# A state space scan regrouped by four tokens, inside a two-mixer transformer kernel on Trainium2

## What is computed

```python
mag, ang = exp(a_re * dt), a_im * dt            # 32 groups of 64 complex states
lb_re, lb_im = mag * cos(ang), mag * sin(ang)
bu = einsum('bsgh,gph->bsgp', u, bb)            # bb complex, made of lb, a and b
state[t] = lb * state[t - 1] + bu[t]            # complex, for 256 tokens t
y = einsum('bsgp,ghp->bsgh', re(state), c_re) - einsum(..., im(state), c_im) + d_skip * u
y = gelu(y); y = y * sigmoid(y @ w_glu + b_glu)
mix = concat([rmsnorm(y), rmsnorm(attention)]); x = x + rmsnorm(mix @ w_out)
```

## Time and profile before

| | |
|---|---|
| Median of 3 runs | 1364.04 us (1362.24 to 1364.82) |
| The profiled execution, its own time | 1365.96 us |
| Its span, first to last instruction | 1364.0 us |
| Mean granted TensorE clock | 0.977 |
| Busy: PE, DVE, ACT, POOL | 92%, 78%, 43%, 12% |
| Second mixer, first state product to first projection product | 1016.1 to 1136.9 us |

### The profile page before, as it was taken

One profiled execution on the slowest core, in us unless ns is written; L12 is line 12 of the kernel. 1 busy time (PEld: TensorE's weight loads), 2 busy tenths in 40 slices (PEclk: granted clock), 3 DMA queues, 4 the chain that ended last, 5 costly groups with the idle time before them and its releaser, 6 DMA issues.

```text
span 1364.0 us, 23503 instructions
## 1 busy us (share of the span) xinstructions
PE 1256.5 (92%) x9783; PEld 1193.4 (87%) x9783; DVE 1067.2 (78%) x1625; ACT 592.1 (43%) x843; POOL 163.2 (12%) x221
## 2 busy tenths in 40 slices
PE   0799998998999998999989989999988879899998
PEld 0699998987999998999989879999976557799997
DVE  6899998776888767999987768998679887755554
ACT  3434334565434444433355754433442326633332
POOL 0011110000011400111100000000018760000000
PEclk9999999998999998999999989999999989899999
DMA  9799997441788653999974415545612213455441
GB/s 357 306 361 352 361 357 297 139 140 41 298 334 325 235 191 111 359 371 359 347 275 145 134 72 210 199 163 215 241 64 86 68 33 108 162 190 187 186 186 47
DMA packets 66089, 293.70 MB, mean 215 GB/s; under 512 B 7616, under 2 KB 8896, under 8 KB 51904
## 3 DMA queue, kind: packets, MB, share of 16 engines
q1 hardware_dynamic: 47552, 225.09, 45.6%
q0 software_dynamic: 18432, 67.12, 12.3%
HBM read 291.13 MB, written 1.05 MB: 214 GB/s over the span
## 4 chain that ended last, share of the span: by engine, by line
PE 78%; DVE 15%; ACT 4%; issue 2%; DMA 1%; POOL 0%; POOLq 0%; DVEq 0%; SPq 0%; ACTq 0%
PE gu_bank L584 15%; PE gu_bank L582 15%; PE gu_bank L583 15%; PE y_bank L582 6%; PE y_bank L583 6%; PE y_bank L584 6%; PE t_bank L582 2%; PE t_bank L584 2%; PE t_bank L583 2%; DVE ysc L2004 2%; DVE dn_lo L1553 2%; PE gu_bank L604 2%; PE gu_bank L605 1%; PE gu_bank L608 1%; PE gu_bank L555 1%
## 5 line engine op out<-in xcount | busy, mean ns | idle before, releaser
L582 PE MATMUL gu_bank<-hT_hi,gu_hi 128*128 128x256 f32 x1668 | 462.0, 277 | 1.0 <-DVE hT_lo L1539 1.0
L584 PE MATMUL gu_bank<-hT_hi,gu_lo 128*128 128x256 f32 x1668 | 461.9, 277 | 0.0
L583 PE MATMUL gu_bank<-hT_lo,gu_hi 128*128 128x256 f32 x1668 | 461.7, 277 | 0.0
L582 PEld LDWEIGHTS gu_bank<-hT_hi,gu_hi 128*128 128x128 f32 x1668 | 312.9, 188 | 2.6 <-issue 0.9
L583 PEld LDWEIGHTS gu_bank<-hT_lo,gu_hi 128*128 128x128 f32 x1668 | 313.1, 188 | 0.8
L584 PEld LDWEIGHTS gu_bank<-hT_hi,gu_lo 128*128 128x128 f32 x1668 | 313.1, 188 | 0.0
L1558 DVE TENSOR_TENSOR gu_lo<-raw_gu,gu_hi 128x2048 fp32r<-128x2048 f32 x105 | 241.2, 2300 | 36.2 <-ACT gu_hi L1160 32.5
L1173 ACT ACTIVATE sg<-gu_bank 128x256 f32<-128x256 f32 x110 | 42.3, 385 | 519.1 <-PE gu_bank L584 519.1
L1160 ACT ACTIVATE gu_hi<-raw_gu 128x2048 fp32r<-128x2048 f32 x100 | 191.0, 1910 | 5.0 <-DMA raw_gu<-ffn_gu 4.9
L1451 DVE SCALAR_TENSOR_TENSOR stage<-stage,c_row 128x1024 f32<-128x1024 f32 x136 | 160.0, 1220 | 0.0
L1584 DVE TENSOR_TENSOR prod<-sg,gu_bank 128x256 f32<-128x256 f32 x110 | 46.2, 420 | 132.8 <-ACT sg L1173 132.4
(11 more groups left out here) (388 smaller groups left out, 2312.0 us busy)
## 6 DMA issues: line engine op xcount, KB each, us to landing
raw_gu<-ffn_gu SPq DMA_DIRECT2D x110, 1024.0 KB, 6.6
stage<-ada POOLq DMA_DIRECT2D x128, 512.0 KB, 7.3
raw_dn<-ffn_dn SPq DMA_DIRECT2D x110, 512.0 KB, 3.8
ring<-mix_w SPq DMA_DIRECT2D x72, 512.0 KB, 3.5
pro<-ada SPq DMA_DIRECT2D x8, 512.0 KB, 8.7
stage<-ada SPq DMA_DIRECT2D x8, 512.0 KB, 13.9
x<-x_in SPq DMA_DIRECT2D x1, 1024.0 KB, 13.5
wg<-mix_w SPq DMA_DIRECT2D x2, 512.0 KB, 4.8
```

The source lines that it names most:

```text
L582: pe.matmul(to, a[0], b[0], start=start, stop=False)
L583: pe.matmul(to, a[0], b[1], start=False, stop=False)
L584: return pe.matmul(to, a[1], b[0], start=False, stop=stop)
```

## The change

With z = lb, four tokens make one step: state[4m+3] depends on state[4m-1] by z to the fourth and on the four inputs between by z cubed, z squared, z and 1. VectorE makes `bbk` (the input weights times powers 0 to 3) and `czk` (the output weights times powers 0 to 4) in `next_power`, beside the fourth feed-forward part, in 15 pieces in place of 10; the tables shrink to 64 steps and lie in `row_b` and in `cz`. TensorE turns `bbk` in 32 transposes, and ScalarE copies them, in eight copies, into `win`, which lies in `raw_gu`. `near_weights` makes the effect of the 0 to 3 tokens before within a group, as matrices `near` on u; ScalarE copies these into blocks of a matrix of zeros, and VectorE's `near_skip` adds the skip term. `inputs()` makes all states' inputs at once, in four banks; `scan(u)` on VectorE serves four tiles in one go, with the turn back, which GpSimd did; of GpSimd's work in the mixer only memsets stay (`near` and the keys). `outputs(u)` puts 32 small products and four with `near` into one bank, from which ScalarE's gelu reads directly. The tokens of u lie by place in the group (j) and group (m); the copy out of `u` and the gelu reorder them. The attention has four buffers for its probabilities in place of two, and the gating products stand between its stages. The waits between engines change with it (`head_bank`, two banks for column tiles from the fifth on, the loads of the last feed-forward part's first two blocks after `bu_ps`). ScalarE copies `win` 0 and 1 before the root of L1316, 2 and 3 after it, 4 to 7 after tile 2.

Cut to its core (one `...` line for each piece left out, equal indents removed):

```diff
+LIFT = 4
+MT = S // LIFT
...
+bbk = sb(ctx, "bbk", [P, 2, LIFT, ST, 32])
+czk = sb(ctx, "czk", [P, 2, LIFT + 1, ST, 32])
...
+ecos = row_b[:, :].rearrange("p (s m) -> p s m", s=ST)
+esin = cz[:, :, :, :, :].rearrange("p r s g h -> p (r s g h)").rearrange("p (s m) -> p s m", s=ST)
+decay = gate_b[:, :].rearrange("p (s m) -> p s m", s=ST)
+wg = bbk[:, :, :, :, :].rearrange("p r k s c -> p (r k s c)")[:, 0:UT * 512].rearrange("p (c n) -> p c n", c=UT)
+win = raw_gu[:, :, :].rearrange("p r (u k n) -> p r u k n", u=UT, k=LIFT)
...
-    first_blocks(2 * FB * l + FB)
-units(mix2_w, 0, range(RING, 19), mixer2_used)
-sp_.wait_ge(sc2_ps, HEADS2)
+        for n in (FB - 2, FB - 1):
+            sp_.wait_ge(dn_lo_done, 3 * FB + n + 1)
+            load_dn(3 * FB + n + 2, n % 2)
+    else:
+        first_blocks(2 * FB * l + FB)
+units(mix2_w, 0, range(RING, 8), mixer2_used)
+sp_.wait_ge(near_ps, 1)
 for n in range(2):
     sp_.dma_start(wg[:, 2 * n:2 * n + 2, :], mix2_w[UNITS2 + n].rearrange("p (c n) -> p c n", c=2)).then_inc(wg_loaded, 16)
-units(mix2_w, 0, range(19, UNITS2), mixer2_used)
+units(mix2_w, 0, range(8, 16), mixer2_used)
+sp_.wait_ge(bu_ps, 1)
+for n in range(2):
+    load_gu(4 * FB + n, n)
+units(mix2_w, 0, range(16, UNITS2), mixer2_used)
...
+def input_weights(which):
+    for n, u in enumerate(which):
+        for r in range(2):
+            for k in range(LIFT):
+                last = pe.transpose(yb[2 * n + r][:, tok(k)], bbk[:, r, k, 4 * u:4 * u + 4, :].rearrange("p s c -> p (s c)"), ident)
+            last.then_inc(win_ps, 1)
...
+def near_weights():
+    pe.wait_ge(tile_out, base + 3)
+    for u in range(UT):
+        for r in range(2):
+            for s in range(4):
+                last = pe.matmul(tb[0][group(s), P * u:P * (u + 1)], bbk[:, r, 0, 4 * u + s, :], czk[:, r, 0:LIFT, 4 * u + s, :],
+                                 start=r == 0, stop=r == 1)
+    last.then_inc(near_ps, 1)
...
+def inputs():
+    pe.wait_ge(win_out, 2 * UT)
+    pe.wait_ge(u_out, UT)
+    for u in range(UT):
+        for r in range(2):
+            for j in range(LIFT):
+                for s in range(4):
+                    last = pe.matmul(yb[s][:, P * u + MT * r:P * u + MT * (r + 1)], win[group(s), r, u, LIFT - 1 - j, :],
+                                     u2[group(s), u, MT * j:MT * (j + 1)], start=j == 0, stop=j == LIFT - 1)
+    last.then_inc(bu_ps, 1)
+def outputs(u):
+    to = tb[u % 2]
+    if u == 0:
+        pe.wait_ge(near_done, UT)
+        pe.wait_ge(tile_out, base + 4)
+    elif u >= 2:
+        pe.wait_ge(gelu_done, u - 1)
+    pe.matmul(to[:, 0:S], zero[:, 0:1].to_broadcast([P, P]), zero[:, 0:1].to_broadcast([P, S]), start=True, stop=False)
...
+    for lag in range(1, LIFT):
+        pe.matmul(to[:, MT * lag:S], near[:, u, lag, :], u2[:, u, 0:S - MT * lag], start=False, stop=False)
+    pe.wait_ge(states_done, 2 * u + 2)
     for r in range(2):
+        for j in range(LIFT):
+            for s in range(4):
+                pe.matmul(to[group(s), MT * j + 1:MT * (j + 1)], czk[:, r, j + 1, 4 * u + s, :], mc[:, u % 2, r, MT * s:MT * (s + 1) - 1], start=False, stop=False)
+    last = pe.matmul(to[:, 0:S], near[:, u, 0, :], u2[:, u, :], start=False, stop=True)
...
+pe.wait_ge(win_out, 4)
+input_weights((2, 3))
 col_tile(3)
-pe.wait_ge(bb_done, 2)
...
+near_weights()
 pe.wait_ge(x_tok_copied, 4)
...
+inputs()
+for n in range(5, 9):
+    col_tile(n)
+outputs(0)
+col_tile(9)
+outputs(1)
+col_tile(10)
+col_tile(11)
+outputs(2)
+for m in range(4):
+    value_unit(m)
+    if m == 1:
+        outputs(3)
...
+pair(scores, 0)
+pair(scores, 1)
+glu(0)
+pair(turn2, 0)
+glu(1)
+pair(scores, 2)
+pair(head_out2, 0)
+pair(turn2, 1)
+glu(2)
+pair(scores, 3)
+pair(head_out2, 1)
+pair(turn2, 2)
+glu(3)
+pair(head_out2, 2)
+pair(turn2, 3)
+pair(head_out2, 3)
...
+    if n == 4:
+        act.wait_ge(near_zero, 1)
+        act.wait_ge(near_ps, 1)
+        for s in range(4):
+            rows_ = slice(32 * s, 32 * s + 32)
+            act.activation(near[rows_, :, :, rows_].rearrange("p u k c -> p (u k) c"),
+                           tb[0][rows_, :].rearrange("p (n c) -> p n c", c=32), ACT.Copy).then_inc(near_out, 1)
+    if 0 < n < 11:
+        split2(n + SLOTS + 1)
...
+    act.wait_ge(c_ps, u + 1)
+    act.activation(by_place(y2[:, u, :]), tb[u % 2][:, 0:S].rearrange("p (j m) -> p j m", j=LIFT), ACT.Gelu_apprx_tanh).then_inc(gelu_done, 1)
...
 gelu(1)
+split2(15)
+gelu(2)
+gelu(3)
 table(ACT.Exp)
+for t in range(TT):
+    act.wait_ge(tile_ps, base + 13 + t)
+    act.activation(v2[:, t, :], zb[t][:, :], ACT.Copy).then_inc(tile_out, 1)
...
+def next_power(a, k, sign):
+    wide = [P, ST, 32]
+    o1, o2 = (to[:, :, :].rearrange("p a b -> p (a b)").rearrange("p (s c) -> p s c", s=ST) for to in (ma, mb))
+    re, im = (lam[:, r, :].unsqueeze(2).to_broadcast(wide) for r in range(2))
+    step.did(dve.tensor_tensor(o1, a[:, 0, k - 1, :, :], re, ALU.mult))
+    step.then(dve.tensor_tensor(o2, a[:, 1, k - 1, :, :], im, ALU.mult))
+    step.then(dve.tensor_tensor(a[:, 0, k, :, :], o1, o2, ALU.subtract if sign > 0 else ALU.add))
...
 def tables(n):
     if n == 0:
+        start_lift()
+    elif n < 4:
+        next_power(bbk, n, 1)
+    elif n < 8:
+        if n == 4:
+            start_c()
+        next_power(czk, n - 3, -1)
+    elif n == 8:
         start_tables()
+    elif n == 9:
+        level(0)
+        level(1)
+    elif n < 14:
+        level(n - 8)
+    elif n == 14:
+        step.settle()
+        decays()
...
+def near_skip():
+    for u in range(UT):
+        dve.wait_ge(near_out, 4)
+        dve.scalar_tensor_tensor(near[:, u, 0, :], ident, lc[:, B_SKIP + u:B_SKIP + u + 1], near[:, u, 0, :], ALU.mult, ALU.add).then_inc(near_done, 1)
+def scan(u):
+    dve.wait_ge(bu_ps, 1)
+    for s in range(4):
+        bu = yb[s][:, P * u:P * (u + 1)].rearrange("p (r n) -> p r n", r=2)
+        for to, table in ((ma, ecos), (mb, esin)):
+            dve.tensor_tensor(to[:, :, MT * s:MT * (s + 1)], bu, table[:, 4 * u + s, :].unsqueeze(1).to_broadcast([P, 2, MT]), ALU.mult).then_inc(bu_used, 1)
+    dve.wait_ge(bu_used, 8 * (u + 1))
     step.did(dve.tensor_tensor(vin[:, 0, :], ma[:, 0, :], mb[:, 1, :], ALU.add))
     step.then(dve.tensor_tensor(vin[:, 1, :], ma[:, 1, :], mb[:, 0, :], ALU.subtract))
+    size = decay[:, 4 * u:4 * u + 4, :].rearrange("p s m -> p (s m)")
     for r in range(2):
+        step.did(dve.tensor_tensor_scan(ysc[:, r, :], size, vin[:, r, :], 0.0, ALU.mult, ALU.add))
+    step.settle()
+    for to, table in ((ma, ecos), (mb, esin)):
+        turn = table[:, 4 * u:4 * u + 4, :].rearrange("p s m -> p (s m)").unsqueeze(1).to_broadcast([P, 2, S])
+        step.did(dve.tensor_tensor(to[:, :, :], ysc[:, :, :], turn, ALU.mult))
+    step.settle()
+    if u >= 2:
+        dve.wait_ge(c_ps, u - 1)
+    dve.tensor_tensor(mc[:, u % 2, 0, :], ma[:, 0, :], mb[:, 1, :], ALU.subtract).then_inc(states_done, 1)
+    dve.tensor_tensor(mc[:, u % 2, 1, :], ma[:, 1, :], mb[:, 0, :], ALU.add).then_inc(states_done, 1)
+    dve.wait_ge(states_done, 2 * u + 2)
+lo(5)
+lo(6)
+scan(0)
+near_skip()
+lo(7)
+lo(8)
+scan(1)
+lo(9)
+lo(10)
+scan(2)
+lo(11)
+lo(12)
+scan(3)
+for m in range(13, 17):
+    lo(m)
+for h in range(4):
+    maxima(h)
+lo(17)
```

More of the change, by code:

```diff
@@ L500, in _ @@
             pool.wait_ge(masks_loaded, 16)
[L501 removed]
+            step.did(pool.memset(bbd[:, :, :, :, :], 0.0))
             step.then(pool.memset(cz[:, :, :, :, :], 0.0))
@@ L967, in _ @@
             col_tile(4)
-            pe.wait_ge(tile_out, base + 4)
+            near_weights()
             pe.wait_ge(x_tok_copied, 4)
-            inputs(0)
-            inputs(1)
-            for s in range(ST):
-                if s < 7:
-                    col_tile(5 + s)
-                elif s < 11:
-                    value_unit(s - 7)
-                if s >= 1:
-                    outputs(s - 1)
-                if s + 2 < ST:
-                    inputs(s + 2)
-                for stage, first in ((head_out2, 11), (turn2, 10), (scores, 8)):
-                    if s >= first and (s - first) % 2 == 0:
-                        stage(s - first)
-                        stage(s - first + 1)
@@ L986, in _ @@
-            outputs(ST - 1)
-            for stage in (turn2, head_out2):
-                stage(HEADS2 - 2)
-                stage(HEADS2 - 1)
-            pe.wait_ge(wg_loaded, 32)
-            pe.wait_ge(bu_used, 2 * ST)
-            def glu(e, c):
-                pe.wait_ge(gelu_done, c + 1)
-                last = pe.matmul(yb[e][:, 0:S], wg[:, c, tok(e)], y2[:, c, :], start=c == 0, stop=c == UT - 1)
-                if c == UT - 1:
-                    last.then_inc(glu_ps, 1)
+            inputs()
@@ new lines, in _, with glu @@
+            for n in range(5, 9):
[10 more added lines that the diff above has]
+                    outputs(3)
+            def glu(e):
+                if e == 0:
+                    pe.wait_ge(wg_loaded, 32)
+                for c in range(UT):
```

(28 more changed lines are left out.)

224 lines of the change are left out of this document (98 added, 126 removed).

## The result

The changed kernel takes 1343.12 us (median of 4 runs, 1341.99 to 1344.06), the kernel before beside it 1364.41 us (1362.24 to 1364.82). The ratio is 0.984, 95% interval 0.9825 to 0.9855: 21.3 us faster, where 7.2 us were forecast.

A forecast was written before the change was run, and what follows sets the result against it. VectorE was taken to bound the state loop. The heads end 7.7 us sooner, the tail gains 1.2 and half clock costs 1.7: net 7.2 us, from 1364.04 to 1356.8 us as a median; range 1344 to 1381.

The forecast's parts named there:

- I read the difference as GpSimd and VectorE holding each other up: State-tile loop: VectorE's instructions cost more beside GpSimd, a pair of scans 1.68 us against 1.27; gain counted only through the sum.
- The part before: Before the state loop: copies 0.5 us and 16 transposes 1.7 us, so the first state product starts 2.2 us later.
- I take half of the upper bounds for the first two: near_weights and inputs: half of the one-after-another times 6.8 and 28.2 us, so 3.4 and 14.1 us.
- Rival B: Small products: groups really run side by side, near 1.7, inputs 7.0, outputs' part 1.7 us; 10.4 us better, 1346.4; chance 0.20.
- C: Small products: nothing overlaps, 22.7 us worse, 1379.5; placed in the inputs, decided from 0.082 us per record on; chance 0.20.
- For the third I take 2.1 us: The 32 small products of each output: 2.1 us between bounds 0.9 and 3.4, making an output 4.2 us.
- The two waits: Column tile 7 waits 2.7 us for VectorE's scan and split; outputs(2) waits 3.7 us for the bank gelu(0) frees.
- With 5 us of waits for ScalarE: Attention with gating products: 16.7 and 6.9 us plus 5 us of waits, as the turns had, 28.6 us.
- D: Every record has a starting floor whatever its size; at 0.07 us, 14.5 us worse, 1371.3; chance 0.11.
- E: TensorE's granted clock stays at 1.2 GHz through the small products: 25.9 us worse, 1382.7; chance 0.04.
- Would cost only 1.5 us: Case that VectorE stays slow without GpSimd: costs only 1.5 us, in the wait for column tile 7.
- What moves and costs nothing: Feed-forward table pieces (VectorE 5 us behind after seven powers) and reordered loads on SP's queue: 0, up to 2 us without cover.

The follow-up runs named there:

- b_pool_tiny: The kernel before, with GpSimd's four operations per state tile on 8 of 256 columns: 1344.75 us, ratio 0.9852 to the kernel before.
- a_pool_noise: The changed kernel with 40 GpSimd multiplications of 512 elements added from the end of inputs on: 1367.18 us, ratio 1.0019 to the kernel before.
- a_again: The changed kernel run once more, unedited: 1342.95 us, ratio 0.9838 to the kernel before.
- a_in_two: The changed kernel, with the products of inputs alternating between two groups of rows only: 1343.41 us, ratio 0.9843 to the kernel before.
- a_gelu_early: The changed kernel, with ScalarE's gelu(0) and gelu(1) right behind its work for column tiles 9 and 10: 1334.33 us, ratio 0.9789 to the kernel before.
- a_best4: The changed kernel with gelu(0) and gelu(1) earlier, all four gating products in the tail, lo(18) later: 1331.88 us, ratio 0.9757 to the kernel before.
- a_in_serial: The changed kernel, with four neighbouring products of inputs in the same group of 32 rows: 1359.81 us, ratio 0.9959 to the kernel before.

## Why the prediction was wrong, step by step

The direction and the mechanism were right, and the size was 14 us too small. The steps by their order:

- **"I read the difference as GpSimd and VectorE holding each other up"**: right, shown by b_pool_tiny and a_pool_noise. But the sum used it only for VectorE's own prices. What the 6.4 us step cost the kernel was never estimated by itself; b_pool_tiny shows some 17 us, and 3 for GpSimd's own last turn, which would have been a check on a forecast of 7.2.
- **The part before**: from the first sum to the first product of the stage the trace shows 0.7 us more (27.8 against 27.1), not 2.2. ScalarE's copies hid, and the rest is the full clock of this one execution; at half clock, as in a_again (29.2 us), it is 2.1 us more, what the sum had. So this term was right, and its gain in the profile was luck.
- **"I take half of the upper bounds for the first two"** is the step that failed most. 3.4 and 14.1 us were 1.9 and 7.35, with 1.55 us of "issue" in the middle that nobody had in the sum: 7.0 us. The reason given, that the two records of one product share a group and can't overlap, so that only half can be gained, is refuted: records cost 0.029 us in four groups and 0.108 in one. In a_in_two each of the two groups even takes a record every 0.068 us. Rival B had near_weights and the inputs right and its chance of 0.20 too low; for the outputs' small products it took 1.7 us where the sum's own lower bound was 0.9, and with that bound it would have been 1343.2. C had the right price for the wrong order: no row of before showed neighbours in different groups, and the source's order was the evidence to weigh. (C would decide from 0.083 us per record on, not 0.082.)
- **"For the third I take 2.1 us"**: 1.02 us at full clock. An output is 2.3 to 2.5 us, not 4.2; outputs(2) took 4.4 us at half clock. The shape changes cost little. The seven column tiles were 0.1 us each too cheap: the first and last of the earlier trace rows lie 2.79 us apart for 23 steps, 0.121 each.
- **The two waits**: outputs(2) waited 4.2 us (3.7 forecast) for gelu(0), by the chain that was named; column tile 7 waited 1.1 us (2.7). That the first wait would also bring half clock for the next 5 us was missed, as was the 1.6 us of half clock behind the stop in the inputs; both are hidden in the 50.8 us, and a_gelu_early brings the first out.
- **"With 5 us of waits for ScalarE"**: there were 0.3 us. With gating products between the stages TensorE was busy 23.8 of 24.0 us, and this is the attention's 4.6 us. a_best4, without them, waits 3.3 us for ScalarE in that stretch (the first two rows of its waits and 0.9 us in short ones), so they hide most of it. That the 5.9 us of the earlier trace rows came from stages squeezed between state steps on a late VectorE is my reading; no run tests it.
- **The tail**: right, 9.4 us from the heads to the projection (9.1), 7.4 of them idle, and 2.1 us lost to the clock (1.7).
- **D and E**: no floor at 0.07 us; records start 0.016 us apart, and the granted clock was 1.00 in the windows from 1018 to 1026 us, over `inputs`. But 1.2 GHz, E's level, did come behind the stop in them and in outputs(2).
- **"Would cost only 1.5 us"**: wrong by more than ten times under the load of a_pool_noise, which is denser than GpSimd's was before.
- **What moves and costs nothing**: right. TensorE was busy 167.3 of the 168 us of the feed-forward part, as before, and a_gelu_early shows no wait for unit 8. (Seven powers at 0.6 us put VectorE 4.2 us behind, not 5.)

## What to carry to other kernels

Order short f32 products so that neighbours lie in different groups of 32 rows or columns; two alternating row groups already gave 3.2 times here, and the same products in one group took three quarters of the gain away. Before pricing a move off GpSimd, look which VectorE instructions read two SBUF tensors beside it: most paid 0.66 to 0.84 us each, those with an operand in PSUM nothing. A wait of TensorE can cost more than its length: 4.2 us were followed by 5 us at 1.2 GHz, and a wait of 3.6 us by half clock in five executions of ten. So fill it with work that is due anyway, and do not read a clock, or a shift of 1 or 2 us, from one trace.

## What the runs showed that was not expected

- Contention is a price per instruction, not a rate: one of 128 elements and one of 1024 paid 0.75 and 0.81 us beside GpSimd's instructions of 1.37 us. Small instructions suffer most.
- The same kernel, with the same wait of 3.6 us, met its first column tiles at 2.4 GHz in one execution and at 1.2 GHz in another. What decides it no run here shows.
- The inputs' 256 records stop once, in each trace behind the same 250th record, for 1.2 to 3.2 us of "issue" (1.55 in the changed kernel, none in a_in_serial). No run here tells what it is; it lies ahead of `bu_ps` and so on the path of the first scan.
- Two row groups do nearly as well as four (0.034 and 0.029 us per record), while four column groups reach 0.016 us (with 63 columns and 32 columns of weights, against 64 and 128). What sets the 0.029 was not tried.
